# Moving the last third of a modulation from TensorE products to VectorE row sums

## The reference

```
sh1, sc1, g1, sh2, sc2, g2 = split(silu(cond) @ ada_w + ada_b, 6)      # per group, 6 x 1024 values
h = rmsnorm(x) * (1 + sc1) + sh1
proj = h @ w_in                       # latent attention, recurrent block, differential attention
merged = gate0 * o_mla + gate1 * o_lru + gate2 * o_diff    # gates: sigmoid(h @ w_merge + b)
x = x + g1 * (merged @ w_out)
h2 = rmsnorm(x) * (1 + sc2) + sh2
x = x + g2 * moe(h2)                  # top 4 of 32 experts, SwiGLU; all experts' weights are read
```

## Time and profile before

| | |
|---|---|
| median of 3 runs | 1677.37 us (1675.06 to 1678.94) |
| the profiled execution | 1678.11 us |
| its span, first to last instruction | 1676.5 us |
| mean granted clock of TensorE | 0.954 |
| busy: TensorE, VectorE, ScalarE | 1523.0 us (91%), 568.9 us (34%), 257.7 us (15%) |
| read from HBM | 542.06 MB, 325 GB/s over the span |

### The profile page before, as it was taken

The page is one execution under the profiler, slowest core; times in us unless marked ns, Lnnn a source line. Parts: engine busy times, 40 slices in busy tenths (PEclk is TensorE's granted clock), DMA queues, the critical chain, the costliest instruction groups (busy, mean ns, idle before and its releaser), DMA issues. The chain is left out here.

```text
span 1676.5 us, 20150 instructions
## 1 busy us (share of the span) xinstructions
PE 1523.0 (91%) x8000; PEld 894.0 (53%) x8000; DVE 568.9 (34%) x1459; ACT 257.7 (15%) x579; POOL 3.8 (0%) x6
## 2 busy tenths in 40 slices
PE   5999999989999989596879999999899999897968
PEld 2756788764454444232438567887643544343424
DVE  2378336334521111110134682363446212111112
ACT  2034122030000000000020342220300100000001
POOL 0000000000000000000000000000000000000000
PEclk8999999999999999897989999999999999998979
DMA  9753613877899999999986436229679999999994
GB/s 394 262 194 129 289 76 126 348 311 301 366 431 430 429 430 431 430 431 431 429 337 221 185 144 271 95 107 373 286 301 387 430 430 429 430 431 430 431 431 208
DMA packets 48710, 545.86 MB, mean 326 GB/s; under 512 B 12704, under 2 KB 13472, under 8 KB 15584
## 3 DMA queue, kind: packets, MB, share of 16 engines
q1 hardware_dynamic: 39488, 539.95, 77.0%
q10 hardware_dynamic: 9120, 4.53, 1.0%
HBM read 542.06 MB, written 2.40 MB: 325 GB/s over the span
## 5 line engine op out<-in xcount | busy, mean ns | idle before, releaser
L876 PE MATMUL ps<-ring,arena 128*32 128x512 f32 (+2 forms) x1216 | 292.5, 620 | 32.5 <-DMA arena<-exp_w_dram 24.9
L876 PE MATMUL ps<-arena 128*64 128x512 f32 (+1 forms) x896 | 235.7, 627 | 14.1 <-DMA ring<-exp_w_dram 14.1
L876 PEld LDWEIGHTS ps<-ring,arena 128*32 128x32 f32 (+2 forms) x1216 | 89.3, 130 | 189.6 <-issue 188.1
L689 PE MATMUL ps<-hT,ring 128*128 128x256 f32 x768 | 171.4, 379 | 0.0
L896 PE MATMUL ps<-ring,arena 128*32 128x512 f32 (+1 forms) x704 | 153.3, 647 | 13.9 <-DMA ring<-exp_w_dram 13.9
L689 PEld LDWEIGHTS ps<-hT,ring 128*128 128x128 f32 x768 | 144.1, 190 | 19.4 <-issue 1.0
L689 PE MATMUL ps<-arena,ring 128*128 128x256 f32 x640 | 144.6, 380 | 2.9 <-ACT arena L1082 1.6
L837 PE MATMUL ps<-arena,hT 128*128 128x128 f32 x896 | 119.5, 290 | 12.2 <-DVE arena L1572 12.2
L837 PEld LDWEIGHTS ps<-arena,hT 128*128 128x128 f32 x896 | 112.2, 204 | 33.3 <-issue 17.3
L896 PE MATMUL ps<-arena 128*64 128x512 f32 (+2 forms) x352 | 105.5, 636 | 26.8 <-DMA ring<-exp_w_dram 26.8
L876 PEld LDWEIGHTS ps<-arena 128*64 128x64 f32 (+1 forms) x896 | 68.6, 130 | 113.1 <-issue 113.1
(11 more groups left out here) (282 smaller groups left out, 1385.9 us busy)
## 6 DMA issues: line engine op xcount, KB each, us to landing
ring<-exp_w_dram SPq DMA_DIRECT2D x118, 2048.0 KB, 23.4
arena<-exp_w_dram SPq DMA_DIRECT2D x77, 2048.0 KB, 25.3
ring<-front_dram SPq DMA_DIRECT2D x58, 2048.0 KB, 10.4
ring<-front_dram SPq DMA_DIRECT2D x2, 1152.0 KB, 17.8
ring<-front_dram SPq DMA_DIRECT2D x2, 1024.0 KB, 18.2
ring<-front_dram SPq DMA_DIRECT2D x2, 640.0 KB, 29.5
xT<-x_in_dram SPq DMA_DIRECT2D x1, 1024.0 KB, 5.0
arena<-lru_gate_w_dram ACTq DMA_DIRECT2D x4, 256.0 KB, 15.8
```

What stands on the lines that cost most here:

```text
L689: last = mm(out, slot[:, k, cols], src[:, k, :], start=k == 0, stop=k == nk - 1)
L876: last = mm(ps[c, h, :], xTg[:, 4 * part + k, c], w[i][:, k, h * 512:(h + 1) * 512], start=False, stop=True, skip_group_check=True)
```

## The change

The last third of the modulation is computed on VectorE. The conditioning vectors of both groups are loaded into every partition (cB, arena columns 21344 to 23391, inside place 7), by a broadcast on ScalarE's queue during the input projection; ScalarE makes tanh of half of it and VectorE the product, which is twice silu. Positions 25 to 28 now hold the matrix turned: 4 x 128 columns on partitions, 1024 rows along the free dimension. For each of 16 column blocks and 2 groups one instruction multiplies 1024 weights with cB and sums them into one column of modT (32 row sums). Two of these stand behind each of the heads u = 8 to 11, one ahead of each of the eight last projection merges, two ahead of each of the eight output merges. `add_bias` and `norm_factor` follow. Every fourth block signals ada_v, which frees a ring slot; SyncE waits for it where it waited for TensorE's products, and requests place 7 behind all sums. TensorE's products, the four transposes and the two evacuations of the last third go.

```
             for r in range(3):
                 if S_ADA[r] <= pos < S_ADA[r] + 4:
-                    return ada_mm, 4 * r + pos - S_ADA[r] + 1
+                    return (ada_v if r == 2 else ada_mm), 4 * (r % 2) + pos - S_ADA[r] + 1
...
                     held_part(6)
-                    held_part(7)
                     sp_.wait_ge(ot_mm, 4)
...
                     sp_.wait_ge(f_mm, len(MERGE))
                     sp_.wait_ge(f_dv, 32)
+                    sp_.wait_ge(ada_v, 4)
+                    held_part(7)
                     held_part(9)
...
-                    ada_products(2, 0)
                     odif_transposes(11)
-                    merge(8)
-                    ada_transposes(2, 1)
-                    merge(8)
+                    merge(16)
...
                     A(lam[:, 4:6], lam[:, 0:2], ACT.Exp).then_inc(lam_exp, 1)
+                    act.dma_start(cB.rearrange("p g n -> p (g n)"), cond_rows.broadcast_to((P, G * D))).then_inc(
+                        ld_cb, 16)
+                    act.wait_ge(ld_cb, 16)
+                    for g in range(G):
+                        A(at(D * g, D), cB[:, g, :], ACT.Tanh, scale=0.5).then_inc(cb_tanh, 1)
...
-                    modulation(2, 0)
                     odif_evac(11)
...
+                    def modulation_dots(n):
+
+                        for _ in range(n):
+                            i, g = dots[0] // G, dots[0] % G
+                            dots[0] += 1
+                            if i % 4 == 0 and g == 0:
+                                arrived(dve, S_ADA[2] + i // 4)
+                            slot = ring[:, (S_ADA[2] + i // 4) % RING, :].rearrange("p (c k) -> p c k", k=D)
+                            last = V.tensor_tensor_reduce(out=cjunk, in0=slot[:, i % 4, :], in1=cB[:, g, :],
+                                                          scale=0.5, scalar=0.0, op0=ALU.mult, op1=ALU.add,
+                                                          accum_out=modT[:, 32 + i, g:g + 1])
+                            if i % 4 == 3 and g == 1:
+                                last.then_inc(ada_v, 1)
+                                dve.wait_ge(ada_v, i // 4 + 1)
+                            else:
+                                link(last)
+
+                    def add_bias(c):
+
+                        link(V.tensor_tensor(modT[:, c, :], modT[:, c, :],
+                                             vec[:, V_ADAB + c.start:V_ADAB + c.stop][:, :, None].broadcast_to((P, 8, G)),
+                                             ALU.add))
...
                         V.tensor_copy(projm[:, u % 2, c0:c0 + w], ps[:, u, 0:w]).then_inc(win_v, 1)
+                    for g in range(G):
+                        dve.wait_ge(cb_tanh, g + 1)
+                        V.scalar_tensor_tensor(out=cB[:, g, :], in0=at(D * g, D), scalar=1.0, in1=cB[:, g, :],
+                                               op0=ALU.add, op1=ALU.mult).then_inc(cb_prod, 1)
                     dve.wait_ge(win_v, 4)
...
                             last.then_inc(on_v, 1)
-                    merge(8)
-                    modulation(2, 1)
-                    merge(8)
+                            if u == 8:
+                                dve.wait_ge(cb_prod, 2)
+                            modulation_dots(2)
+                    for _ in range(8):
+                        modulation_dots(1)
+                        merge(1)
+                    add_bias(slice(32, 40))
+                    norm_factor(A2, 32, V_N2)
+                    for _ in range(8):
+                        modulation_dots(2)
+                        merge(1)
+                    add_bias(slice(40, 48))
```

More of the change, by code:

```diff
@@ L133, in later_uses, with build @@
     return len(range(s, PRE, RING)) - 1
-def build(nc, x_in, cond_in, consts, vecs, rows, front, lru_gate_w, router_w, exp_w1, exp_b1, exp_w2, exp_b2,
+def build(nc, x_in, cond_in, cond_rows, consts, vecs, rows, front, lru_gate_w, router_w, exp_w1, exp_b1, exp_w2, exp_b2,
           cache_ckv, cache_krope, cache_dk, cache_dv, y_out, new_ckv, new_krope, new_lru, new_dk, new_dv):
@@ L232, in build @@
         c_dv = at(20832, 512)
+        cB = at(21344, G, D)
+        cjunk = at(21344 + G * D, D)
         more = [at(SLOT, SLOT), at(21088, SLOT), at(E0, SLOT), at(0, SLOT)]
@@ L302, in build @@
                                                  ("ada_mm", "ada_sb", "ada_tr", "prep", "mod_rdy"))
+        ld_cb, cb_tanh, cb_prod, ada_v = sem("cond_rows_in"), sem("cond_tanh"), sem("cond_silu"), sem("ada_dve")
         sp_abs, sp_ln, lam_exp = sem("sp_abs"), sem("sp_ln"), sem("lam_exp")
@@ L1218, in _, with norm_factor @@
                                     ALU.add).then_inc(prep, 1)
+                    def norm_factor(out, sc, nrm):
+                        V.scalar_tensor_tensor(out=out[:, :, :], in0=modT[:, sc:sc + 8, :], scalar=1.0,
+                                               in1=vec[:, nrm:nrm + 8][:, :, None].broadcast_to((P, KC, G)),
+                                               op0=ALU.add, op1=ALU.mult).then_inc(mod_rdy, 1)
+                    dots = [0]
+                    def modulation_dots(n):
[17 more added lines that the diff above has]
+                                             ALU.add))
                     def modulation(r, bank):
@@ L1229, in modulation @@
                         else:
[L1230 to L1233, removed]
+                            norm_factor(A1, 8, V_N1)
                     dve.wait_ge(ada_mm, 4)
@@ L1786 @@
         for j in range(4):
-            front[S_ADA[r] + j] = blocks(a["ada_w"][:, 2 * j * P:2 * (j + 1) * P], r * 2048, 2048)
+            if r == 2:
+                c0 = (4 * r + j) * 512
+                front[S_ADA[r] + j] = a["ada_w"][:, :, c0:c0 + 512].transpose(0, 2, 1).reshape(
+                    L, 4, P, D).transpose(0, 2, 1, 3).reshape(L, P, -1)
+            else:
+                front[S_ADA[r] + j] = blocks(a["ada_w"][:, 2 * j * P:2 * (j + 1) * P], r * 2048, 2048)
     for p, (c0, n) in zip(S_IN, IN_SLICES):
@@ L1799 @@
         "cond_in": cond.T.reshape(KC, P, G).transpose(1, 0, 2),
-        "consts": constants(np), "vecs": vecs, "rows": rows,
+        "cond_rows": cond.reshape(1, -1), "consts": constants(np), "vecs": vecs, "rows": rows,
         "front": np.concatenate(front, axis=2),
```

## The result

The changed kernel takes 1715.95 us (median of 4 runs, 1709.91 to 1718.67) against 1677.82 us for the kernel before beside it (1675.06 to 1678.94). The ratio is 1.022, with a 95% interval of 1.0192 to 1.0248: slower by 38 us, where 24 were forecast. 1716 us lies at the upper end of the range (1686 to 1717 us) and above the 1708 us at which the likeliest account alone ended. The profiled execution is the slowest of the four, 1718.67 us with a span of 1717.0 us, 40.5 us more than that of before.

A forecast was written before the change was run, and what follows sets the result against it. Expert weight streaming was taken as the bound, so delays reaching pass 0 count: 9.3 us per layer (18.6) plus 5.2 at the front, 23.8 us on 1678.1, forecast 1701 us, range 1686 to 1717 us.

The forecast's parts named there:

- the likeliest account alone: Whole kernel: the forecast of 1701 us without the rivals, from 1692 to 1708 us, chance 0.62.
- rival A: Front: the broadcast lands after 21 us, the convolution waits 10.1 us in each layer; 1716 us, chance 0.12.
- Row sums: VectorE: 32 sums of 1024 elements per layer, 1.22 us each, 1.26 with the gap, 40 us for all 32.
- Rival D: VectorE: sums run at half rate, 2.33 us each, 40 us more per layer; 1762 us, chance 0.03.
- Heads: Heads 8 to 11: each pair of sums costs the next head 1.5 us, three heads 4.5 us per layer.
- Projections and outputs: Last merges: 2.1 us per projection against TensorE's 1.75, ending 1.8 us late; output sums covered, 3.17 against 3.48 us.
- of its 7.07 us about 1.3 are left: Behind the last head: its later norm leaves 1.3 of the 7.07 us of removed TensorE work as gain.
- The weight queue: SyncE's in-order queue: expert loads stand behind the last sums, pass 0 waits 6.8 us and starts 8.6 us late.
- B (weights in time): Ahead of pass 0: the loads are not waited for, layers late by the merges alone; 1686 us, chance 0.13.
- C (the stream swallows it): Expert stage: the late loads fill idle DMA pauses, the layer's end stays; 1678 to 1682 us, chance 0.10.
- After the wait: Behind pass 0's wait: half clock loses 1.7 us, 1.0 us of routing wait comes back, per layer.
- The conditioning vector: Front: the 1 MB broadcast, tanh and product delay the convolution; TensorE waits 2.6 us, 5.2 us for both layers.

The follow-up runs named there:

- Experiment 3: Changed kernel with each head's pair of row sums moved from behind its norm to between its two merges: 1702.75 us, ratio 1.0139.
- Experiment 6: Kernel of experiment 4 with TensorE's removed products put back at their old place, their result unused: 1683.39 us, ratio 1.0032 against the kernel before.
- experiment 7: Kernel of experiment 4 with three second-branch projections moved ahead of three gates: 1674.68 us, ratio 0.9975 against the kernel before.
- experiment 1: Changed kernel with only SyncE's requests reordered, to the order in which places come free: 1698.44 us, ratio 1.0112.
- experiment 5: Kernel before with only SyncE's weight requests made late, no row sums and no broadcast: 1703.03 us, ratio 1.0132.
- experiment 4: Changed kernel with the edits of experiment 1, experiment 2 and Experiment 3 together: 1679.62 us, ratio 1.0001 against the kernel before.
- experiment 8: Kernel of experiment 7 with three sums at each of the last four heads and four ahead of the projections: 1672.87 us, ratio 0.9962 against the kernel before.
- experiment 2: Changed kernel with the tanh written to other columns and VectorE's product with it placed behind the convolution: 1713.05 us, ratio 1.0206.

## Why the prediction was right, and where its sum fell short

The direction and the places held, and with two exceptions (the load of position 29, the half clock behind short waits) the mechanisms. The sum was 23.8 us where 38 were measured (40.5 between the two profiled executions). That 1716 us lies in the range is partly luck: the range reached beyond 1708 us to take in rival A, which did not happen. By its own steps:

- *Row sums.* 1.22 us forecast and measured, at intervals of 1.26. The Trainium skill (Vector Engine (DVE) Microarchitecture Reference, Points that are easy to get wrong) puts an accumulating instruction with two f32 sources in SBUF at half throughput; this trace does not agree, at 1220 ns for 1024 elements. The page says it of one instruction shape (S2S2D2_STT), and the trace, which lists the sums as CUSTOM_DVE_ANT_0, does not say whether they have it. Rival D falls.
- *Heads.* The wait of the transposes came as 1.40, 1.40 and 1.91 us where 1.5 was worked out, but the three heads lost 1.6, 1.9 and 2.4 us: 0.5 us of the 1.9 go beside the recorded wait, at the matmuls just before and behind it, which stand further apart. Experiment 3 shows that the place of the pair, and not the number of sums, made it.
- *Projections and outputs.* 2.06 us per product for 2.1, and outputs covered at 27.86 us: right. The step that failed stands between heads and projections: "of its 7.07 us about 1.3 are left". The last head's norm was seen as the one thing that the removed products covered. They also covered the load of position 29, whose slot is free only when the second branch's last projection is done. Requested at 311.18, it is waited for until 318.69: 1.90 us, and 1.54 in the second layer; before, 0.8 us of waiting for ScalarE stood there. Experiment 6, with the products put back, and experiment 7, with the load requested at 289.68 us, both remove this wait.
- *The weight queue.* Right in place and order. The waits are 8.56 and 7.01 us, for 6.8. Experiments 1 and 5 show it from both sides: 17.5 us given back by the order of the requests, 23 us made by late requests alone. Rivals B (weights in time) and C (the stream swallows it) fall: the request that opens the stream moved by 22.45 and 39.96 us, and the end by 40.5. One reading was wrong without a consequence for the sum: six requests were indeed made from 305 us on, but for places 2, 3, 4, 6, 7 and 8; places 5, 0 and 1 followed from 324.29 to 353.55.
- *After the wait.* 1.0 us came back at the routing, as forecast. The half clock cost 2.2 and 1.7 us, for 1.7. Here is the larger mis-sized term: the half clock was counted once per layer, behind the long wait, and given to no short one. In the first layer the recurrent gates took 6.46 us for 3.62, one projection product in the last head 3.68 for 1.89, and the projections of the third branch 17.80 us, for 15.27 with the same sums at full clock in experiment 6. That is 7.2 us more; in the second layer the same three places cost 1.7 us. The trace before already had such places: behind 3.56 us of waiting for the second norm, TensorE's clock was 0.68 from 360.06 to 364.40.
- *The conditioning vector.* Waits of 3.36 and 0.39 us for the 2.6 forecast in both layers. The broadcast landed after 16.0 us, between the 13.5 and 21.4 of the earlier trace rows. What differs is the request: in the second layer it goes out at 913.09 us, 3.5 us ahead of the input projection's products of L660 (916.56), in the first at 53.55, 0.2 us behind their start (53.40). Taking the first layer's sum twice was wrong here. Rival A, which gave the measured time (1716 us), is wrong as a mechanism: the front lost 7.0 us and not 20.

Between the profiled executions 16.7 us are missing from the sum (40.5 less 23.8). The missing terms are the half clock behind short waits (7.2 + 1.7 = 8.9 us), the heads (5.9 us per layer for 4.5, so 2.8 us), the load of position 29 (3.4 us of waiting, less the 1.6 us for ScalarE that it replaced: 1.8 us), 2.0 us more of waiting ahead of pass 0 with 0.5 us more of half clock behind it, and the 2.9 us outside the layers' stretches (the three shifts named under the table). The front's waits are 1.5 us less than forecast. Together this is 17.4 us; the remaining 0.7 us are not assigned.

Why a removal of 14.1 us of TensorE work gains nothing even when everything else is put right (experiment 4) follows from 6, 7 and 8: the removed work was cover for two waits, it kept the clock up, and some 2.2 us per layer went to the sums that set the projections' pace (experiment 6 against the kernel before; 2.3 us came back in experiment 8, with four sums there instead of eight). Where other products took its place, the kernel was 5.1 us faster than the one before, with the sums spread 6.9 us. How much of this the removal itself brings is open without the new order on the kernel before. Open are also the size of experiment 2, and 2.5 of the 3.4 us between the layers: from the request that opens the first layer's stream to the next layer's first loads it took 389.7 us before and 392.2 after, and values between these in the other eight kernels, in no order that an edit explains. Experiment 4 shows what such drifts do: there the stream opens 1.9 and 1.2 us earlier than before, and the profiled execution ends 0.7 us later.

## What to carry to other kernels

Work that seems removable from the critical engine may be the cover of a wait on another engine and of a load in flight: list all that becomes ready during it, and put other work there before counting its time as saved. When a buffer's last reader moves to another engine, look at the in-order queue that refills it: everything behind that wait is late with it, and putting the requests whose buffers are already free first costs one line. Put added work of a slower engine into a wait that it already has, and not ahead of what the critical engine waits for.

## What the hardware showed that was not expected

Behind short waits the half clock cost up to as much again as the wait. In the changed kernel the granted clock was 0.50 from 86.77 to 90.80 us, behind 3.36 us without a product, and 0.50 from 318.69 to 322.50, behind 1.22 and 1.90 us of waiting with only 0.44 us of work between. In experiment 7 the same projections follow a wait of 0.80 us and have the clock 1.00 in their first 4 us, and take 15.28 us in all. But a wait does not decide alone: behind 1.91 us at the last head the clock was 0.52 in the first layer (3.68 us for eight matmuls), and behind 1.90 us at the same place in the second layer the same eight took 1.99 us, at full clock. Experiment 6 shows the same: behind 2.21 us ahead of the output products the clock was 0.58 from 325.60 to 329.60 in the first layer and 1.00 behind the same 2.21 us in the second. What else decides, these runs don't show.
